# Sample state products of a hybrid decoder layer on stacked fp32r halves, and the first four feed-forward slabs together

## The reference

```python
a = rmsnorm(h, norm_g[l, 0]) * (1.0 + sc1) + sh1
# HGRN2, 16 heads, chunks of 32 (a sample is one chunk of 4):
S = exp(G_last)[..., None] * S + einsum('bhsd,bhsv->bhdv', k_ * exp(G_last - G), i_)
# gated delta rule, 32 value heads on 16 key heads, chunks of 64:
v_new = u - einsum('bhtd,bhdv->bhtv', w, S)
S = exp(g_last)[..., None] * S + einsum('bhsd,bhsv->bhdv', k_ * exp(g_last - gam)[..., None], v_new)
mix = (sigmoid(gate_a) * (o_hg @ w_out_hg) + sigmoid(gate_b) * (o_gdn @ w_out_gdn)) @ w_o
h = h + g1 * rmsnorm(mix, norm_g[l, 1])
a = rmsnorm(h, norm_g[l, 2]) * (1.0 + sc2) + sh2
h = h + g2 * rmsnorm(square(relu(a @ w_up)) @ w_down, norm_g[l, 3])
```

## Time and profile before

| | us |
|---|---|
| three runs | 3514.32, 3516.87, 3517.03 |
| median | 3516.87 |
| the profiled execution | 3517.61 |
| its span | 3516.1 |
| PE busy | 3445.2 (98%) |
| DVE busy | 2298.1 (65%) |
| ACT busy | 1849.5 (53%) |
| POOL busy | 854.8 (24%) |
| mean granted PE clock | 0.994 |

### The profile page before, as it was taken

One profiled execution on the slowest core, in us unless ns is written; L12 is line 12 of the kernel. 1 busy time (PEld: TensorE's weight loads), 2 busy tenths in 40 slices (PEclk: granted clock), 3 DMA queues, 4 the chain that ended last, 5 costly groups with the idle time before them and its releaser, 6 DMA issues.

```text
span 3516.1 us, 77141 instructions
## 1 busy us (share of the span) xinstructions
PE 3445.2 (98%) x24605; PEld 3167.9 (90%) x24605; DVE 2298.1 (65%) x4411; ACT 1849.5 (53%) x3831; POOL 854.8 (24%) x995
## 2 busy tenths in 40 slices
PE   8999999999999999999999999999989999999998
PEld 2799999998889999998899999999869889999998
DVE  8766666646677777776677777646666665555555
ACT  6554545455545555555555555454665555344454
POOL 3122222201145545450244554412000000000000
PEclk9999999999999999999999999999999999999999
DMA  9555555568844434448644444468755775555554
GB/s 354 174 161 146 159 145 160 145 190 264 241 110 117 113 110 125 120 119 265 182 135 112 117 111 110 135 187 255 229 172 150 229 229 163 167 162 166 160 163 140
DMA packets 884548, 588.11 MB, mean 167 GB/s; under 512 B 23426, under 2 KB 816036, under 8 KB 884164
## 3 DMA queue, kind: packets, MB, share of 16 engines
q1 hardware_dynamic: 857828, 510.50, 50.6%
q0 software_dynamic: 26624, 76.41, 7.6%
HBM read 545.83 MB, written 40.99 MB: 167 GB/s over the span
## 4 chain that ended last, share of the span: by engine, by line
PE 69%; DVE 1%; issue 1%; ACT 1%; DMA 0%; DVEq 0%; ACTq 0%; SPq 0%
PE acc L653 18%; PE acc L655 17%; PE acc L654 17%; PE bank L844 2%; PE bank L857 2%; PE bank L894 2%; PE bank L878 1%; PE bank L665 1%; PE bank L666 1%; PE bank L915 1%; PE bank L926 1%; PE bank L940 1%; PE bank L816 1%; PE bank L787 1%; PE bank L792 0%
## 5 line engine op out<-in xcount | busy, mean ns | idle before, releaser
L1616 DVE TENSOR_TENSOR wlo<-raw,whi 128x512 fp32r<-128x512 f32 x1799 | 1304.5, 743 | 814.3 <-ACT whi L1094 799.3
L1094 ACT ACTIVATE whi<-raw 128x512 fp32r<-128x512 f32 x1799 | 1095.0, 627 | 835.1 <-PE acc L655 798.3
L653 PE MATMUL acc<-ahi,whi 128*128 128x288 f32 x4112 | 1288.3, 313 | 14.4 <-DVE alo L2133 9.0
L654 PE MATMUL acc<-alo,whi 128*128 128x288 f32 x4112 | 1214.7, 295 | 0.0
L655 PE MATMUL acc<-ahi,wlo 128*128 128x288 f32 x4112 | 1210.8, 294 | 0.0
L653 PEld LDWEIGHTS acc<-ahi,whi 128*128 128x128 f32 x4112 | 774.9, 188 | 37.3 <-issue 29.6
L654 PEld LDWEIGHTS acc<-alo,whi 128*128 128x128 f32 x4112 | 776.0, 189 | 13.3 <-issue 11.5
L655 PEld LDWEIGHTS acc<-ahi,wlo 128*128 128x128 f32 x4112 | 775.4, 189 | 0.0
L653 PE MATMUL acc<-ohi,whi 128*128 128x288 f32 x1792 | 532.3, 297 | 2.2 <-DVE wlo L1616 1.9
L654 PE MATMUL acc<-olo,whi 128*128 128x288 f32 x1792 | 528.7, 295 | 0.0
L655 PE MATMUL acc<-ohi,wlo 128*128 128x288 f32 x1792 | 527.4, 294 | 0.0
(11 more groups left out here) (438 smaller groups left out, 4480.3 us busy)
## 6 DMA issues: line engine op xcount, KB each, us to landing
raw<-in_w_in SPq DMA_DIRECT2D x386, 512.0 KB, 4.1
raw<-in_w_ada SPq DMA_DIRECT2D x192, 512.0 KB, 4.9
raw<-in_w_up SPq DMA_DIRECT2D x128, 512.0 KB, 4.3
raw<-in_w_down SPq DMA_DIRECT2D x128, 512.0 KB, 4.0
raw<-in_w_out_gdn SPq DMA_DIRECT2D x64, 512.0 KB, 5.1
raw<-in_w_o SPq DMA_DIRECT2D x34, 512.0 KB, 4.8
raw<-in_w_out_hg SPq DMA_DIRECT2D x32, 512.0 KB, 5.4
g_S<-in_state_gdn POOLq DMA_DIRECT2D x32, 512.0 KB, 6.6
```

Source lines behind the costliest of these rows:

```text
L653: mm(bank[:, 0:T], whi[:, s, r, :], hi[:, kt, :], start=(kt == 0), stop=False, skip_group_check=True)
L654: mm(bank[:, 0:T], whi[:, s, r, :], lo[:, kt, :], start=False, stop=False, skip_group_check=True)
L1094: f(whi[:, s], raw[:, r], ACT.Copy).then_inc(sg["hi_made"], 1)
L1616: tt_(wlo[:, s], raw[:, r], whi[:, s].bitcast(F32), SUB).then_inc(sg["lo_made"], 1)
```

## The change

Three independent parts.

**Samples' state products.** Token rows are made four times instead of once (tiles `h_k4`, `h_i4`, `g_ck4`, `g_uTs` repeat the 32 sample columns, so that the turn fills 128 rows). ACT rounds the 128 rows to fp32r (`h_st`, `g_kst`, `g_vst`), and DVE replaces some row groups by what the rounding left, so that keys stand as high, high, low, low and values as high, low, high, low (HGRN: s=2; delta net: keys at s=3, values at s=17, which POOL now waits for). One fp32r product over 128 rows then sums the four combinations. The masks `cm4` and the spread tiles cover 128 rows. In HGRN the spread product moves from s=8 to s=9.

**Feed-forward.** The first four w_up slabs are computed together: a piece is now one k-tile of four slabs, loaded as rows of 2 KB, and PE adds to four banks (`acc0`, `acc1`, R6, R7). The splits of its pieces move between the steps that make `ahi` and `alo`. The residual groups become 4, 4, 4, 2, 2, and part of ACT's scaling moves behind the squares.

**Sums and end.** In w_o ACT squares before it drains; the last square goes to PE by a product of its own, not through DVE. At the end every group is added right after it is scaled.

```diff
@@ tensor, HGRN
                 if s == 8:
                     pe.wait_ge(sg["h_tok"], n + 1)
-                    pe.wait_ge(sg["h_spread"], n + 1)
+                    pe.wait_ge(sg["h_wide"], 1 + n + 1)
...
+                if s == 9:
+                    pe.wait_ge(sg["h_spread"], n + 1)
                     for a in range(2):
-                        last = mm(R[2 + a][:, :], htoks[:, 0, :], hiXs[:, 4 * a:4 * a + 4, :].rearrange("p c v -> p (c v)"),
+                        last = mm(R[2 + a][:, :], hst[:, 0, :], hiXs[:, 4 * a:4 * a + 4, :].rearrange("p c v -> p (c v)"),
@@ tensor, delta net
                 if s in (18, 22):
...
-                        last = mm(R[4 + a][:, :], gkls[:, e, :], gvX[:, 4 * a:4 * a + 4, :].rearrange("p b v -> p (b v)"),
+                        last = mm(R[4 + a][:, :], gkst[:, e, :], gvX[:, 4 * a:4 * a + 4, :].rearrange("p b v -> p (b v)"),
@@ scalar, delta net, at s == 46 and at s == 15
+                    for e in range(2):
+                        last = f(gkst[:, e, :], R[2][:, 2 * P:3 * P], ACT.Copy, scale=gsc[:, e, 5:6])
 +                    f(gvst[:, :, :], R[5][:, 0:2 * P].rearrange("p (e v) -> p e v", v=P), ACT.Copy)
@@ vector, HGRN
+                if s == 2:
+                    dve.wait_ge(sg["h_tok"], n + 1)
+                    for rows_, k in ((slice(2 * NS, P), 0), (slice(NS, 2 * NS), 1), (slice(3 * NS, P), 1)):
+                        last = tt_(hst[rows_, k, :], R[3][rows_, k * P:(k + 1) * P], hst[rows_, k, :].bitcast(F32), SUB)
+                    last.then_inc(sg["h_at"], 1)
@@ vector, delta net
+                if s == 17:
+                    dve.wait_ge(sg["g_vns"], n + 1)
+                    for rows_ in (slice(NS, 2 * NS), slice(3 * NS, P)):
+                        last = tt_(gvst[rows_, :, :], R[5][rows_, 0:2 * P].rearrange("p (e v) -> p e v", v=P), gvst[rows_, :, :].bitcast(F32), SUB)
+                    last.then_inc(sg["g_vlo"], 1)
@@ gpsimd, delta net
-                pool.wait_ge(sg["g_vns"], n + 1)
+                pool.wait_ge(sg["g_vlo"], EARLIER8 + n + 1)
...
-                    pt(gvX[0:NS, :, :], gvns[0:NS, e, :].unsqueeze(1).to_broadcast([NS, NB, P]),
-                       cm4[:, :].unsqueeze(2).to_broadcast([NS, NB, P]), MUL).then_inc(sg["g_vx"], 1)
+                    pt(gvX[:, :, :], gvst[:, e, :].bitcast(F32).unsqueeze(1).to_broadcast([P, NB, P]),
+                       cm4[:, :].unsqueeze(2).to_broadcast([P, NB, P]), MUL).then_inc(sg["g_vx"], 1)
@@ tensor, feed-forward
+            def four_slabs(at, hi, lo, made):
...
+                for kt in range(KT):
+                    s = at.slot(kt, SPLIT)
+                    pe.wait_ge(sg["lo_made"], at.pieces_before(kt) + 1)
+                    pe.wait_ge(sg[made], kt + 1)
+                    for k, bank in enumerate((acc[at.bank(0)], acc[at.bank(1)], R[6], R[7])):
+                        mm(bank[:, 0:T], whi[:, s, k, :], hi[:, kt, :], start=(kt == 0), stop=False, skip_group_check=True)
+                        mm(bank[:, 0:T], whi[:, s, k, :], lo[:, kt, :], start=False, stop=False, skip_group_check=True)
+                        last = mm(bank[:, 0:T], wlo[:, s, k, :], hi[:, kt, :], start=False, stop=(kt == KT - 1), skip_group_check=True)
@@ vector, feed-forward
             for j in range(1, KT // 2):
                 feed(j)
                 feed_lo(j - 1)
-                if j == 5:
-                    split_lo(pos(S_FF, 0, 2), 0)
+                if j > 1:
+                    split_lo(first, 2 * j - 4)
+                    split_lo(first, 2 * j - 3)
@@ vector, start of HGRN
-                nc.vector.memset(hiXs[rows_, :, :], 0.0)
@@ vector, end
-            gated_scaled(0)
-            for i in range(1, len(OUT)):
+            for i in range(len(OUT)):
                 gated_scaled(i)
-                result(i - 1)
-            result(len(OUT) - 1)
+                result(i)
```

More of the change, by code:

```diff
@@ L533, in _ @@
             mixed_loop(sp, mixed(wo, 0), S_WO)
[L534 removed]
+            four_slabs(pos(S_FF, 0, 2), wup, 0)
+            with sp.Fori(2, KT // 2) as n:
+                pair(wup, 0, 0)(ff_pos(0, n), n)
             mixed_loop(sp, mixed(wdown, 0), S_DOWN0)
@@ L1441, in _, with squares, scaled_rows, feed @@
             norm(1)
[L1442 to L1446, removed]
+            def squares(i):
+                m, size = GROUPS[i]
+                act.wait_ge(sg["w_h"], i + 1)
+                f(wsq[:, m:m + size, :], res[:, m:m + size, :], ACT.Square).then_inc(sg["w_hsq"], 1)
+            def scaled_rows(first, end):
+                for m in range(first, end):
+                    f(mix[:, m, 0:TP], res[:, m, 0:TP], ACT.Copy, scale=mod_of(4, m)[:, 0:1]).then_inc(sg["w_hs"], 1)
+            squares(0)
+            scaled_rows(0, 4)
+            squares(1)
+            scaled_rows(4, 6)
+            squares(2)
+            squares(3)
+            squares(4)
+            scaled_rows(6, 10)
             norm(2)
             first = pos(S_FF, 0, 2)
-            for j in range(KT // 2):
+            def feed(j):
                 act.wait_ge(sg["b_a"], EARLIER + j + 1)
@@ L1454, in _ @@
                 f(ahi[:, 2 * j:2 * j + 2, TP:T], mix[:, 2 * j:2 * j + 2, TP:T], ACT.Copy).then_inc(sg["b_hi"], 1)
-                if j == 3:
-                    split_hi(first, 0)
+            for j in range(KT // 2):
+                feed(j)
+                if j < 3:
+                    scaled_rows(10 + 2 * j, 12 + 2 * j)
+                if j > 0:
+                    split_hi(first, 2 * j - 2)
+                    split_hi(first, 2 * j - 1)
+            split_hi(first, KT - 2)
+            split_hi(first, KT - 1)
             def up_slab(g, n, k, made=0):
@@ L1968, in delta_prev @@
             def delta_prev(s, n, slot):
+                if s == 3:
+                    low = slice(2 * NS, P)
+                    dve.wait_ge(sg["g_khi"], EARLIER + n + 1)
+                    for e in range(2):
+                        last = stt(gkst[low, e, :], R[2][low, 2 * P:3 * P], gsc[low, e, 5:6], gkst[low, e, :].bitcast(F32), MUL, SUB)
+                    last.then_inc(sg["g_klo"], 1)
                 if s == 7:
@@ L2176, in first_down @@
                     down(at, 2 * n, k, (lambda: mod_add(at, n)) if k == MIXED_SLABS - 1 else None)
-            up_slab(0, 0, 0, made=1)
-            up_slab(0, 0, 1)
-            up(0, begun=1)
+            for i in range(4):
+                k = i % 2
+                drained(first, i)
+                dve.wait_ge(sg["f_lo"], EARLIER + 2 * (i // 2))
+                dve.wait_ge(sg["f_hi"], EARLIER + 2 * (i // 2))
+                tt_(tu[:, k, :], tt[:, k, :], tt[:, k, :], MUL).then_inc(sg["f_sq"], 1)
+                dve.wait_ge(sg["f_hi"], EARLIER + i + 1)
+                tt_(olo[:, i, :], tu[:, k, :], ohi[:, i, :].bitcast(F32), SUB).then_inc(sg["f_lo"], 1)
+                split_lo(first, KT + i)
+            up_slab(0, 2, 0, made=4)
+            up_slab(0, 2, 1)
+            up(0, begun=3)
             dve.wait_ge(sg["w_clear"], 3)
```

207 lines of the change are left out of this document (136 added, 71 removed).

## The result

| | before | changed |
|---|---|---|
| median, 13 runs each | 3517.03 us | 3524.68 us |
| range | 3514.32 to 3520.63 | 3520.55 to 3527.76 |
| profiled execution, span | 3516.1 | 3520.6 |
| ratio, 95% interval | | 1.0021 (1.0012 to 1.0029) |

What follows compares the result with a forecast made beforehand. PE, busy for 98% of the span, was taken as the bound. Terms -20.0, -40.0, +40, +14, -6, -1.1, -1.2, -1.1 sum to -15.4 us on 3517.6; less 0.7 to the median, 3501.5 us, range 3474 to 3526.

Steps and rivals of the forecast that it cites:

- Price of the products: Samples' products: each step gives back 1.25 us of PE; HGRN -20.0 us, delta net -40.0 us.
- HGRN's cover: HGRN: spread is ready before its product, cover 2.1 us plus 0.8 us from moving to s=9; cost 0.
- The wait at s=18: Delta net: PE stalls 2.5 us in each of 16 rounds for POOL's spread, +40 us; bounds 1.9 and 4.4 us.
- What the step cost besides: Delta net: second spread, DVE's later work and added copies cost 0, up to 0.2 us per round if tight.
- The new wait: Delta-net passage of the prediction: late subtraction at s=17 stalls PE, +40 us; the other shifted work costs 0.
- The clock: Delta rounds: stall lowers PE's clock in half of the rounds, 8 times 1.75 us, +14 us; bounds 0 and 46 us.
- Rival 1: Delta rounds: the stall is there but the clock holds; 3487 us, chance 0.22.
- Rival 2: Delta rounds: DVE's taps hold up POOL's first spread, stall 4.4 us; 3550 us, partly so about 3525; chance 0.12.
- Feed-forward: First four slabs: first feed step to fourth slab's end takes 30.7 us instead of 36.6, -6 us; bounds -8 and 0.
- w_o and end: w_o: DVE's add leaves the chain, -1.1 us; end: second scaling no longer precedes the first result, -1.2 us.
- Start: Kernel start: two clears of 0.91 us go, ahead of a chain PE waits on; -1.1 us (0 to -3.2).

Runs made afterwards that it cites:

- early_add: Changed kernel with ACT's value copies (s=15) and DVE's subtraction (s=17) moved to s=14, DVE's state additions from s=23 to s=22; 3465.5 us, ratio 0.9856.
- before_wait: Kernel before the change, plus two small DVE operations at s=17 that alter no values and for which POOL's spread waits; 3557.39 us, ratio 1.0107.
- taps_first: Changed kernel with POOL's first spread held back until DVE's taps of s=18 are done; 3570.85 us, ratio 1.0149.
- early_taps: Changed kernel with ACT's value copies and DVE's subtraction moved to s=14, POOL's second spread held until DVE's taps are done; 3470.95 us, ratio 0.9872.
- early_both: Changed kernel with the edits of early_taps and early_add together; 3454.3 us, ratio 0.9823.
- no_delta: Changed kernel with the delta net's part undone, all other parts kept; 3490.05 us, ratio 0.9920.

## Why the prediction was wrong, point by point

- **Price of the products: right.** HGRN heads went from 34.90 to 33.65 us, 1.25 each: the second head's product starts at 201.17, the first's at 167.52. In the delta rounds a step gives 1.25 too. The 128-column weights don't show.

```profile
167.52 0.62 PE L755 MATMUL bank<-h_iXs,h_st 128*128 128x512 f32 x2
...
201.17 0.62 PE L755 MATMUL bank<-h_iXs,h_st 128*128 128x512 f32 x2
```

- **HGRN's cover: right.** No wait stands before that product.
- **The wait at s=18: right in place, cause and size.** Forecast 2.5 us (bounds 1.9 and 4.4), measured 2.37, released by POOL's spread. All 16 rounds have it, the last one for 1.64 us.
- **What the step cost besides: here it failed.** In "The new wait" the working put 0 on everything but the wait: "The second spread of the round starts after the first product and has over 3 us until s=22: cost 0. DVE gets 0.7 us later, but waits for PE's product of s=19 anyhow". The spread was indeed in time for PE. What was not asked is what it does to DVE. In 11 of the 15 rounds with taps both spreads lie on them and the taps take 3.1 us more (in the other four, all with a fall of the clock, one does and they take 1.5 us more). DVE no longer waits for PE's product of s=19 but comes after it, and in the eight rounds without a fall that have taps PE waits 0.43 us at s=21. The sum also counted on PE's wait giving DVE the same time as before, while PE's own work between was being cut by 1.25 us. That is the wait at s=24: PE stands for 0.43 us until DVE's additions are done (early_add). With 0.2 to 0.25 us of drain and refill at each wait, which the sum had not either, this is the +1.91 us of a round where the sum had 0 (-2.5 for the products, +2.5 for the wait): 16 times 1.91 is 30.6 us, the shorter wait of the last round not allowed for. It is the term that turned the sign. The same passage put DVE's work at s=3 at 0; in the first round PE waits 1.74 us for it.
- **The clock: mechanism right, price too high.** Forecast falls in half of the rounds, 1.75 us each, 14 us. The trace has 7 in 16, each beginning within 1.5 us of the end of the wait at s=18, for 3.4 us. Rounds with one are 0.4 to 1.0 us longer than 75.55, but for two that have other waits also. They cost less than the remaining 5.8 us (36.4 - 30.6), as the first round's wait of 1.74 us is in it too; and in these seven rounds the wait at s=21 is not there. One of them, the wait and what follows it at the lower level of 1.2 GHz:

```profile
1071.00:1074.00 3.00, 0.68 (x6) 0.44 (x4) 2.92 (x4) 1.87 (x4) 1.94 (x1) 1.00 0.52 142
1075.30:1078.60 3.30, 3.30 (x17) 3.30 (x16) 3.27 (x4) 1.40 (x3) 1.46 (x1) 0.50 0.02 5
```

  Rival 1, in which the clock holds, is out. The Trainium skill (TensorE: Matmul & The Clock Gate, "Why this matters for your kernels") lets it fall only for gaps longer than this wait. Here waits of 2.2 to 2.4 us sufficed in 7 of 16 rounds, and of 1.80 us in 3 of 16 (before_wait). The measurement decides. The wait at 118 to 121, which the prediction gave as agreeing, was longer than this one, so it said nothing of shorter ones.
- **Rival 2 had the right pair and the wrong victim.** It forecast POOL held up by the taps. POOL's spreads took 1.94 and 1.90 us; the taps paid. Its size for a wait of 4.4 us, 3550 us, is tested by taps_first: 3570.85, with a wait of 4.71 us, the small wait at s=24, and the clock falling every time.
- **Feed-forward: right.** From the first feed step (2642.41) to the end of the fourth slab (2672.47) it takes 30.1 us against 36.6, -6.5 where -6 was forecast. PE's clock was low for the first 3.4 us, as assumed; then PE did not wait.
- **w_o and end: right.** The sum of w_o -1.8 us (from +14.1 to +12.2; forecast -1.1), the end -1.0 (-1.2).
- **Start: wrong, nothing was gained.** Forecast -1.1; the first head's product is 1.2 us late. The wait of 3.2 us at 117 is unchanged (3.19 us), so the cleared tiles were not on its path. The 1.2 us are the clock's: from the end of that wait to the first head's product it was at half for 9.4 us instead of 6.8. The stretch takes 43.5 us before, and 43.4 to 43.5 in three runs with the new start and 6.8 us at half (early_taps, early_both, taps_first). With some 9.5 us at half it takes 44.6 us in the changed kernel, and 44.1 in before_wait, which has the old start.

The sum with the measured differences: -20.2 from the HGRN heads, +1.2 from the start and -3.4 on the way to the second delta round give -22.4; then +36.4 from the delta rounds, -1.8 from w_o, -6.7 from norms and feed-forward and -1.0 at the end: +4.5 us in span (rounding aside). Most of the -3.4 is no gain of the change: between these two starts PE waits 6.7 us in all where the kernel before has 9.7, and in the run no_delta it is 9.7 again.

## What to carry to other kernels

A product that gets cheaper takes cover away from every chain beside it: look not only at whether its inputs arrive, but at who used the time that it gives back. When a step moves in time, look at what it now runs beside, in both directions: here the second spread, 1.9 us of POOL, was in time for PE and cost it nothing directly, but it made DVE's operations beside it 1.5 us longer. Before such a change is given up, move the small steps that feed it into waits that the trace shows: three moves of steps turned 7.7 us of loss into 63 us of gain (3454.3 us against 3517.6).

## What the runs showed of the hardware

- Which of DVE and POOL pays went by who started first in these rounds. In the changed kernel the first of the three taps, cut out by a narrower window, begins 0.22 us behind the spread, lasts 2.06 us where a third of the earlier trace rows is 0.57, and ends 0.34 us after it; the spread keeps its 1.94 us. The operation before (line 1963), which reads one tile and a column of scalars, keeps its 0.38 us, and the spread that starts while it runs keeps its 1.94. Where a split of DVE has started first (early_both, 1210.77 against 1210.87), it keeps its 0.69 us and the spread takes 2.35. The Trainium skill (SBUF — State Buffer, "Who interferes with whom") agrees: an operation of DVE with two SBUF inputs contends with POOL's reads, whoever issues first holds the pair for the whole instruction, and the other is blocked. The prediction had applied that rule to one side only.

```profile
1224.72 2.06 DVE L1966 SCALAR_TENSOR_TENSOR g_ca<-g_U,g_cw,g_ca 128x312 f32<-128x312 f32 x1
```

- Each wait of PE among dense products costs 0.2 to 0.26 us more than the idle time shown (0.53 us for a wait of 0.33 in early_taps, 2.06 us for one of 1.80 in before_wait).
- The clock fell behind waits of 1.8, 2.2 to 2.4 and 4.7 us in 3, 7 and 15 of the 15 rounds that have them; the last rounds' waits of 1.11, 1.64 and 1.65 us brought no fall. It also fell once behind a wait of 1.34 us (before_wait, 1734.19), while it held behind one of 1.43 us in the kernel before (986.99). What decides for the single round stays open.
